# Attention rows 0 to 5 of a hybrid block: projection halves, turned tokens and router placed later in the step order

## The reference

```
u = rms_norm(h, g_mix)
q, k, v, f, B, C, hc = split(u @ w_in)
q, k = rms_norm(q), rms_norm(k)                 # per head of 64, 8 heads
logit[t, s] = q_t.k_s / sqrt(64) + sum of log_sigmoid(f) over s < j <= t      # causal
attn = softmax(logit) @ v
conv = B * conv3(C * hc)                        # depthwise, causal
h = h + concat(headRMS(attn), headRMS(conv)) @ w_out
g = top-1 of 4 expert groups; e = top-2 of the 8 experts in it    # router logits from rms_norm(h)
h = h + sum over the 2 experts of gate * (silu(x @ w_gate[e]) * (x @ w_up[e])) @ w_down[e]
```

## Time and profile before

| | before |
|---|---|
| median of 3 runs | 1252.49 us |
| the profiled execution | 1252.73 us |
| its span | 1251.0 us |
| PE busy | 1127.7 us (90%) |
| DVE busy | 629.8 us (50%) |
| ACT busy | 534.8 us (43%) |
| attention, 371 to 622 us | about 251 us |
| mean granted clock of TensorE | 0.972 |

### The profile page before, as it was taken

How to read it: one execution, slowest core, us unless ns; L and a number is a source line. 1 busy time by engine, 2 the same in 40 slices (tenths; PEclk the granted TensorE clock), 3 DMA queues, 4 the chain that set the end, 5 groups by cost and what they waited for, 6 DMA issues and landing times.

```text
span 1251.0 us, 18120 instructions
## 1 busy us (share of the span) xinstructions
PE 1127.7 (90%) x6677; PEld 853.8 (68%) x6677; DVE 629.8 (50%) x909; ACT 534.8 (43%) x804; POOL 222.7 (18%) x256
## 2 busy tenths in 40 slices
PE   6999999999998999999887999998999998989960
PEld 5999988899995666666666886655555555556530
DVE  6422333234326566665478865555545544445526
ACT  7302141144335445444335864455544554444520
POOL 4000001130300111000132213222222222222110
PEclk9999999999999999999988999999999999999985
DMA  9420015324014332221278999999999999999869
GB/s 266 102 69 1 1 47 189 135 104 136 1 42 111 95 97 76 73 68 68 94 292 324 369 379 404 420 426 405 392 398 391 405 391 398 402 383 398 355 246 366
DMA packets 66250, 291.54 MB, mean 233 GB/s; under 512 B 10696, under 2 KB 36328, under 8 KB 53648
## 3 DMA queue, kind: packets, MB, share of 16 engines
q1 hardware_dynamic: 48176, 243.38, 51.2%
q0 software_dynamic: 16720, 42.65, 9.0%
q10 hardware_dynamic: 1296, 4.72, 1.0%
HBM read 270.62 MB, written 37.92 MB: 247 GB/s over the span
## 4 chain that ended last, share of the span: by engine, by line
PE 59%; DMA 21%; DVE 7%; issue 7%; ACT 4%; SPq 1%; POOL 0%; DVEq 0%; ACTq 0%; POOLq 0%
DMA wg<-in_w_gate 18%; PE ps L1027 10%; PE ps L1028 10%; PE ps L1029 10%; PE ps L1343 4%; PE ps L1345 3%; PE ps L1344 3%; PE ps L1154 3%; PE ps L1122 2%; PE ps L1136 2%; ACT wg_high L1689 2%; DMA y<-expert_rows 2%; PE ps L1357 2%; DVE probs L2102 1%; PE ps L1192 1%
## 5 line engine op out<-in xcount | busy, mean ns | idle before, releaser
L2154 DVE TENSOR_TENSOR wu_low<-wu,wu_high 128x2048 fp32r<-128x2048 f32 x36 | 81.1, 2287 | 54.9 <-ACT wu_high L1689 54.9
L1357 PE MATMUL ps<-wu,xa 128*64 128x512 f32 x224 | 102.1, 598 | 0.0
L1357 PE MATMUL ps<-wg,xa 128*64 128x512 f32 x224 | 102.1, 598 | 0.0
L1689 ACT ACTIVATE wd_high<-wd 128x2048 fp32r<-128x2048 f32 x36 | 66.9, 1906 | 80.6 <-DMA wd<-in_w_down 78.8
L2154 DVE TENSOR_TENSOR wd_low<-wd,wd_high 128x2048 fp32r<-128x2048 f32 x36 | 81.2, 2288 | 35.8 <-ACT wd_high L1689 35.6
L1689 ACT ACTIVATE wu_high<-wu 128x2048 fp32r<-128x2048 f32 x36 | 66.9, 1907 | 67.0 <-DMA wu<-in_w_up 67.0
L2154 DVE TENSOR_TENSOR wg_low<-wg,wg_high 128x2048 fp32r<-128x2048 f32 x36 | 81.0, 2289 | 21.6 <-ACT wg_high L1689 21.6
L2257 DVE TENSOR_TENSOR hid<-sil,ps 128x512 f32<-128x512 f32 x18 | 12.4, 686 | 131.4 <-PE ps L1345 131.4
L1689 ACT ACTIVATE wg_high<-wg 128x2048 fp32r<-128x2048 f32 x36 | 66.9, 1907 | 26.4 <-DMA wg<-in_w_gate 24.8
L967 POOL DMA_INDIRECT expert_rows<-yb,idxs x32 | 47.9, 1497 | 160.1 <-ACT yb L1738 121.8
L1027 PE MATMUL ps<-uh,w_high 128*128 128x342 f32 (+1 forms) x208 | 71.4, 343 | 0.0
(11 more groups left out here) (388 smaller groups left out, 2980.2 us busy)
## 6 DMA issues: line engine op xcount, KB each, us to landing
wg<-in_w_gate SPq DMA_DIRECT2D x32, 2048.0 KB
wu<-in_w_up SPq DMA_DIRECT2D x32, 2048.0 KB, 21.2
wd<-in_w_down SPq DMA_DIRECT2D x32, 2048.0 KB, 20.1
u_rows<-u POOLq DMA_DIRECT2D x16, 512.0 KB, 6.4
y<-expert_rows SPq DMA_DIRECT2D x16, 512.0 KB, 10.3
raw_c<-in_w_in SPq DMA_DIRECT2D x5, 1024.0 KB, 5.7
xin<-in_x SPq DMA_DIRECT2D x8, 512.0 KB, 9.9
zx<-in_x POOLq DMA_DIRECT2D x4, 1024.0 KB, 7.0
```

The lines of the kernel that those rows point to most:

```text
L1357: last = mm(ps[HALF * n:HALF * (n + 1), 7, :], xa[:, k, :], raw[m][:, 1, k, :], start=(k == 0), stop=(k == KT - 1))
L1689: A(flat_half(wh[m][:, :, :], n), flat_half(raw_kf(m, s), n), ACT.Copy).then_inc(w_high[m], 1)
L2154: return V.tensor_tensor(flat_half(wl[m][:, s, :, :], n), flat_half(raw_kf(m, s), n), flat_half(wh[m][:, :, :], n).bitcast(F32), ALU.subtr ...
```

## The change

Rows 6 and 7 keep the old tables; rows 0 to 5 get new ones. For a row `r` of 0 to 5, in steps after `first_step(r)`:

| piece | PE before | PE now | DVE before | DVE now | ACT before | ACT now |
|---|---|---|---|---|---|---|
| W0 | 1c | 1d | 1d | 1d | | |
| W1 | 1d | 2b | 2a | 2c | | |
| URS | | | | | 2a | 2d |
| U2 | | | 2b | 3a | | |
| U0 | 2c | 3b | 2d | 3c | 2d | 3c |
| U1 | 2d | 3d | 3a | 4a | | |
| L | 3c | 4b | 3d | 4b | | |
| LT | 3d | 4c | 4a | 4c | | |

M, G, O, A, AL, RT, S, GT, ASQ, ARS, AH and GE stay. MS, in step 26, moves on PE from before turns 2 and 3 to behind place c. `BEFORE_TURNS` is emptied: 14 fillers fall away.

```diff
-def extras_at(table, step, place):
-    return [(kind, r) for r in reversed(range(NT)) for (rel, at), kind in table.items()
+PE_LATER = {(0, "d"): "M", (1, "d"): "W0", (2, "b"): "W1", (3, "b"): "U0", (3, "d"): "U1",
+            (4, "b"): "L", (4, "c"): "LT", (5, "b"): "G"}
+def extras_at(tables, step, place):
+    return [(kind, r) for r in reversed(range(NT)) for (rel, at), kind in tables[r >= NT - 2].items()
             if at == place and step == first_step(r) + rel and step < UNITS + 2]
...
-BEFORE_TURNS = {("U0", 0): 8, ("U1", 0): 2, ("U0", 1): 4}
+BEFORE_TURNS = {}
...
                 if u >= 2:
                     times_v(u - 2, 0, 2)
-                for kind, i in extras_at(PE_EXTRA, u, "b"):
+                for kind, i in extras_at((PE_LATER, PE_EXTRA), u, "b"):
+                    extra(kind, i)
+                for g in range(2, min(4, n)):
+                    turn(u - 1, g)
+                for kind, i in extras_at((PE_LATER, PE_EXTRA), u, "c"):
                     extra(kind, i)
                 if u == META_STEP:
                     extra("MS", NT - 1)
-                for g in range(2, min(4, n)):
-                    turn(u - 1, g)
-                for kind, i in extras_at(PE_EXTRA, u, "c"):
-                    extra(kind, i)
                 if u >= 2:
                     times_v(u - 2, 1, 2)
```

More of the change, by code:

```diff
@@ L114 @@
 ACT_EXTRA = {(0, "b"): "ASQ", (1, "a"): "ARS", (1, "b"): "AH", (2, "a"): "URS", (2, "d"): "U0", (5, "d"): "GE"}
-def extras_at(table, step, place):
-    return [(kind, r) for r in reversed(range(NT)) for (rel, at), kind in table.items()
+PE_LATER = {(0, "d"): "M", (1, "d"): "W0", (2, "b"): "W1", (3, "b"): "U0", (3, "d"): "U1",
+            (4, "b"): "L", (4, "c"): "LT", (5, "b"): "G"}
+DVE_LATER = {(-1, "d"): "SQ", (0, "a"): "O", (1, "a"): "A", (1, "b"): "AL", (1, "d"): "W0",
+             (2, "c"): "W1", (3, "a"): "U2", (3, "c"): "U0", (4, "a"): "U1", (4, "b"): "L", (4, "c"): "LT",
+             (4, "d"): "RT", (5, "c"): "G", (6, "c"): "GT"}
+ACT_LATER = {(0, "b"): "ASQ", (1, "a"): "ARS", (1, "b"): "AH", (2, "d"): "URS", (3, "c"): "U0", (5, "d"): "GE"}
+def extras_at(tables, step, place):
+    return [(kind, r) for r in reversed(range(NT)) for (rel, at), kind in tables[r >= NT - 2].items()
             if at == place and step == first_step(r) + rel and step < UNITS + 2]
@@ L129 @@
 ACT_TAIL = [("ASQ", R7), ("ARS", R7), ("AH", R7), ("GH", 0), ("GE", R6), ("URS", R7), ("U0", R7)]
-BEFORE_TURNS = {("U0", 0): 8, ("U1", 0): 2, ("U0", 1): 4}
+BEFORE_TURNS = {}
 STREAMED = { ("W0", R7): 13, ("FIRST", R6): 8, ("U0", R7): 3, ("L", R7): 3, ("LT", R7): 2, ("G", R7): 10,
             ("FIRST", R7): 3, ("KIND", 0): 6}
-XJOBS = [job for u in range(UNITS + 2) for place in "abcd" for job in extras_at(PE_EXTRA, u, place)]
+XJOBS = [job for u in range(UNITS + 2) for place in "abcd" for job in extras_at((PE_LATER, PE_EXTRA), u, place)]
 XJOBS.insert(XJOBS.index(("M", META_STEP // PAIRS - 1)), ("MS", NT - 1))
@@ L1301, in _ @@
                     stream(7, 3)
-                for kind, i in extras_at(PE_EXTRA, u, "a"):
+                for kind, i in extras_at((PE_LATER, PE_EXTRA), u, "a"):
                     extra(kind, i)
@@ L1320, in _ @@
                     turn(u - 1, g)
-                for kind, i in extras_at(PE_EXTRA, u, "d"):
+                for kind, i in extras_at((PE_LATER, PE_EXTRA), u, "d"):
                     extra(kind, i)
@@ L1659, in extras @@
             def extras(u, place):
-                for kind, i in extras_at(ACT_EXTRA, u, place):
+                for kind, i in extras_at((ACT_LATER, ACT_EXTRA), u, place):
                     extra(kind, i)
@@ L2116, in extras @@
             def extras(u, place):
-                for kind, i in extras_at(DVE_EXTRA, u, place):
+                for kind, i in extras_at((DVE_LATER, DVE_EXTRA), u, place):
                     extra(kind, i)
```

## The result

The changed kernel takes 1242.79 us (median of 5 runs, 1242.28 to 1246.83) against 1253.56 for the kernel before in the same comparison (1252.26 to 1255.77): a ratio of 0.9922, 95% interval 0.9905 to 0.9939, which is 9.8 us (7.6 to 11.9); the two medians lie 10.8 apart. Compared once more, with the last experiments, the two stood at 1244.03 and 1252.12 us, ratio 0.9936 (0.9920 to 0.9953), 8 us.

The account below looks back on a forecast made before the run. PE's idle time bounds attention, weight reads the experts; 4.8 (W0) + 0.4 (W1) + 4.6 (U0, U1, L, LT) = 9.8 us off 1252.5 gives 1242.7 us. Chance 0.60 for 1237 to 1246; range 1233.5 to 1250.

Parts of the forecast that it names:

- A microsecond of attention is one at the end: Expert loads start behind attention and nothing there hangs on absolute time, so time won in attention shortens the whole equally.
- W0, 4.8 us: PE's waits at W0, rows 0 to 5: half of times_v now covers them, so 7.4 us falls by 4.8.
- W1, 0.4 us: PE's wait at W1: over 2.5 us of work now lies between W0 and W1, so 0.4 us goes.
- U0, U1, L, LT, MS, 8.4 us left: PE's waits and fillers at the token and router pieces: 13.0 us before, some 8.4 after, 4.6 won.
- The parts as a sum: Gains in attention from W0, W1 and the token and router pieces add: 4.8 + 0.4 + 4.6 = 9.8 us.
- The fillers, 3.6 us: 14 filler matmuls ahead of U0 and U1 in rows 0 and 1 take some 3.6 us, counted as removable.
- The clock at nothing: Slow stretches in row 1's W0 and step 26, 1.7 us each: one may go, one grow, together nothing.
- only moves: Rival, chance 0.11: the serial chain through URS and U2 takes gains back; gain 0 to 2.5 us, 1250 to 1252.5.
- all of it goes: Rival, chance 0.10: all 17.2 us of PE waits and 3.6 of fillers vanish; 1231.7, or 1228.3 without slow stretches.
- the slower one: Rival, chance 0.05: DVE waits at L's logits copy, delaying the next scores 2.8 us per row; 7 us slower, 1260.
- The clock rival: Rival, chance 0.14: two or three more slow stretches at 1.7 us each; 1246 to 1248, up to 1249.5.

Follow-up runs that it names:

- e5: The changed kernel with W0 alone of rows 0 to 5 back at 1c on PE; ratio to the kernel before 0.9965.
- e7: The changed kernel with DVE's addition of W1 ahead of its copy of turn 3 instead of behind it; ratio to the kernel before 0.9909.
- e10: The changed kernel with ACT's second exponentials ahead of its copy of turn 2 in the steps holding W1; ratio to the kernel before 0.9928.
- e3: The kernel before with only W0 moved to 1d and W1 to 2a on PE in rows 0 to 5; ratio to the kernel before 0.9999.
- e4: The changed kernel with W0 back at 1c, W1 at 1d and DVE's addition of W1 at 2a; ratio to the kernel before 0.9975.
- e1: The kernel before with only the 14 fillers ahead of U0 and U1 of rows 0 and 1 removed; ratio to the kernel before 1.0007.
- e11: The changed kernel again, unedited, on the same chip as the last experiments; ratio to the kernel before 0.9936.

## Why the prediction was right, point by point

- *A microsecond of attention is one at the end.* It held, with a scatter: 12.6 us won in attention gave 10.4 in the profiled span, and over 13 profiles the rest took 629 to 634 us. Over the twelve comparisons of the table, from no gain to 14 us, the time follows attention within 2.8 us. The reading that the experts are bound by the weights and start behind attention stands: their DMA share is 0.98 in both kernels. The first expert load came at 610.26 us, where I had 612.5.
- *W0, 4.8 us.* Measured 4.7, and e5 undoes it alone: 4.7. By the prediction's terms 1.1, 0.7, 0.3, 0.3, 0.2 and 0 should be left in rows 0 to 5; the trace has 1.28, 0.73, 0.24, 0.29, 0.16 and none.
- *W1, 0.4 us.* Gone.
- *U0, U1, L, LT, MS, 8.4 us left.* Measured 7.8: row 0 1.9 (I had 2.4), row 1 1.6 (1.4), row 2 1.2 (1.1), row 3 0.8 (0.9), row 4 0.67 (0.7), row 5 0.6 (0.8), MS 1.04 (1.1). Turn 3 waits for a copy behind U2 and MS for LT's bank, as I said. But the sum is better than its parts. I put about 3 us on U1, which leaves some 2 for U0 (row 1: U1 1.1, U0 0.3); U1 waits 1.3 and U0 3.1 (row 1: 0.77 and 0.82). And one link was wrong: I let DVE's addition release URS. It does in rows 0 and 4; in rows 1, 2, 3 and 5 ACT's order does (e7, e10), 0.3, 0.8, 0.1 and 0.4 us after the addition. Too much on U1 and too little on U0 cancelled in the sum, which is luck.
- *The parts as a sum.* I worked them out for the whole change and they hold for the whole. As parts they don't stand alone: e3 wins nothing, e4 3 us.
- *The fillers, 3.6 us.* Right as a term of this change, because the hand-worked waits of rows 0 and 1 were set against it. (1.17 us for 4 would make 4.1 for 14; from each group's start to the next instruction they took 1.98, 0.57 and 1.02 us, which is the 3.6.) As time to be won by itself it is nothing (e1).
- *The clock at nothing.* In the first profile this term was off, by 1.7 us won: the first stretch went and the second didn't grow. In e11 it did, to about twice its length, which gives the 1.7 back. The 1.4 us lost behind attention and this 1.7 nearly cancel, and the kernel before ran at 1253.56 us this time, not at 1252.5; so the agreement of 1242.79 with 1242.7 is luck, and 2 us would have been fair.
- *The rivals.* Against "only moves": waits fell by 6.7. Against "all of it goes": 10.5 are left. Against the slower one: no wait ahead of the scores (L1130) stands among the waits. In the steps that hold L, the second take_scores ended 2.3 us or more before PE reached the next scores; the nearest of rows 0 to 5 was row 0's step with U2, at 1.0. The clock rival: two or three more slow stretches came in neither profile of the change. It is the rival least settled, since one did come in a new place in e1 and in e3.

## What to carry to other kernels

When work is moved to cover a wait, list for every engine what now stands between the producer and the consumer, and work the chain through by hand with durations of the trace, the copies and exponentials of the other engines included; here that gave each row's remaining wait to 0.5 us or better, though not always the instruction that it stands at. Pieces that cover each other's chains must be moved together: of the two parts tried, one was worth 3 us and one nothing, the whole 8 to 10. And if shortening a chain on one engine changes hardly any wait, look on the other for an order that ends at the same time or later. Before reading a difference between two profiles, set their slow stretches aside: here they were up to 5 us of attention's length.

## What was not expected of the hardware

- TensorE's slow stretches are not fixed to a wait. Row 1's W0 had one in the kernel before and in e1, behind a wait of 1.3 us, and none behind the same wait in e4 and e5. In e1 one came in row 0, in e3 one in row 2. Behind MS in step 26 it stood in 8 of the 10 profiles with MS there, 3.4 us long in some and 6.9 in others, even in two executions of one kernel (the change and e11); in the 3 with MS elsewhere there was none in attention. A stretch costs 1.7 or 3.4 us by the estimate, and that much executions of one kernel can differ with no change in its order. The Trainium skill (TensorE: Matmul & The Clock Gate, Part 1) says the slow clock is the default and activity releases it; the slow stretches here follow small matmuls or a wait, so the trace agrees, but which of such places is hit it does not tell.
- What removes the stretch behind MS, its distance from LT or its missing wait, was not tried apart.
